# Token-row joints of a two-layer decoder step: pair turns in one run, row 2 ahead of the first unit, diagonals on ScalarE, last pass waiting per weight block

## The chip, the core and the metric

The program runs on one core of a Trainium2 chip. The metric is the device time in microseconds from start to end of one execution; a lower time is better. A profiled execution gives the trace, with the start and duration of every instruction on TensorE (PE), VectorE (DVE), ScalarE (ACT), GpSimd (POOL) and the queue of SyncE (SP).

## What is computed

Two layers over 512 prompt tokens and 64 new tokens (8 sequences of 8). Layer 0 mixes tokens by latent attention (MLA), layer 1 by gated linear attention (GLA). Around each mixer stands a half-step FFN before and after, each with a norm before and after.

```python
def rmsnorm(x, g):
    xf = x.astype(jnp.float32)
    y = xf * lax.rsqrt(jnp.mean(xf * xf, axis=-1, keepdims=True) + EPS)
    return (y * g.astype(jnp.float32)).astype(x.dtype)

def ffn_half(h, g_pre, g_post, w_in, w_out):
    a = rmsnorm(h, g_pre) @ w_in
    gate, up = jnp.split(a, 2, axis=-1)
    return h + FFN_RESID * rmsnorm((jax.nn.silu(gate) * up) @ w_out, g_post)
...
    for i in range(DEPTH):
        g = norm_g[i]
        yp = ffn_half(yp, g[0], g[1], ffn_w_in[i, 0], ffn_w_out[i, 0])
        ...
        yp = yp + rmsnorm(mp, g[3])
        ...
        yp = ffn_half(yp, g[4], g[5], ffn_w_in[i, 1], ffn_w_out[i, 1])
```

The width is 1024, the FFN's inner width 2816. All is float32.

## The kernel before

Six stages run one after the other: ffn, mla, ffn, ffn, gla, ffn. The residual h lies in SBUF by token rows, in five tiles: 0 to 3 of 128 prompt tokens each, 4 with the 64 new ones. They are worked in the order 0, 1, 4, 2, 3. Each stage first needs x = h times the pre-norm gain, transposed, so that the contraction lies on the partitions. The norm's own factor 1/sqrt(sum of squares) is applied later, when results leave PSUM.

Every product of float32 numbers is made from three matmuls of type fp32r: x is split in x_hi and x_lo, the weights in w_hi and w_lo, and hi x hi, lo x hi and hi x lo are added in PSUM. Weights come in blocks of 512 KB through four slots. SyncE loads a block into raw, ScalarE makes w_hi from it (split, L588), GpSimd makes w_lo (L972); for the second block of a stage VectorE does that (w_low, L1106). A slot is loaded again when TensorE has used its block.

A stage ends with its output projection (out_phase). Its output y is made in two halves of 512 columns. In the second half the last three blocks (the last pass) are worked tile by tile, so that the tiles end one after the other. For each finished tile ScalarE squares y (y_square, L602 to L607) and takes the root (y_root, L615); VectorE applies the post-norm gain (y_gain, L1115), inverts the root and adds the result to h (update, L1142). 

A joint is what lies between this and the next stage's dense work:

- **Turning.** TensorE transposes h (turn_pair, L1723, for tiles 0 and 1 together, two k of 128 columns at a time; turn_row, L1735, for the tiles 4, 2 and 3) into PSUM banks 6 and 7. ScalarE makes x_hi from the bank (high, L641), VectorE x_lo (low, L1080). A bank can be turned into again when x_lo has been taken from it.
- **First units.** A unit is one block of weights against 256 tokens (half 0: tiles 0 and 1) or 320 (half 1: tiles 2, 3 and 4). It goes to one of six ring banks. in_head works units 0, 1 and 2 of half 0, and then those of half 1.
- **Factors.** ScalarE squares the rows of h (h_square, L629) and takes the root (h_root, L635 and L636). VectorE inverts it and makes a diagonal matrix (diag, L1152). TensorE spreads it over all partitions with a matmul (spread_factors, L1744 and L1746), and VectorE copies it out (r_pre, L1159 and L1162) ahead of the first unit's eviction (L1195).

The order of instructions on each engine is the order in which they are written; an engine executes its own in that order, and waits for semaphores between. Semaphores are s_hnew (updates of h), s_turn, s_xhi, s_xlo, s_hi and s_lo (weights), s_used and s_unit (blocks and units done), s_evicted (banks freed) and s_diag. In the GLA stage the output projection waits for g_olo, which counts the lowered parts of its input: first the eight of tiles 0 and 1, then the eight of the others with x_s, the part of the new tokens (L1641, L1643).

## Time and profile before

| | us |
|---|---|
| three runs | 2522.61, 2524.40, 2524.88 |
| median | 2524.4 |
| the profiled execution | 2524.44 |
| its span, first to last instruction | 2522.4 |
| TensorE matmuls busy | 2415.3 (96%) |
| TensorE weight loads busy | 2186.4 (87%) |
| VectorE, ScalarE, GpSimd busy | 858.4, 795.7, 834.1 (34%, 32%, 33%) |

The mean granted clock of TensorE is 0.988 of full speed. Matmul rows overlap, since the duration of one has its way through the array in it; the distance between two starts is what one costs. In a waits view a line names who waited for whom; in a timeline the brackets give the idle time of the engine before the group and what ended it. A group of a timeline is merged from consecutive like instructions (x8).

### The profile page before, as it was taken

Reading aid. Unit: us, or ns where it says so; the run is one execution under the profiler, and the core shown is the slowest. Engines: PE = TensorE matmul, PEld = TensorE weight load, DVE = VectorE, ACT = ScalarE, POOL = GpSimd, SP = SyncE. Lnnn points to the kernel's source line nnn. Section 1 sums busy time; section 2 is a strip of 40 time slices with the busy share of each in tenths; the row PEclk is TensorE's granted clock in tenths of the full one; section 3 lists DMA queues with packets and bytes.
Section 4 is the critical chain, followed back from the end, with each engine's and each line's share of the span. In section 5 each row is a group of like instructions: output and inputs, shape, how many; then the busy total and the mean of one; then the engine's idle time right before and its main releaser. Section 6 shows DMA issues by size and latency. Waiting matters only on the chain.

```text
span 2522.4 us, 40060 instructions
## 1 busy us (share of the span) xinstructions
PE 2415.3 (96%) x15520; PEld 2186.4 (87%) x15520; DVE 858.4 (34%) x1923; ACT 795.7 (32%) x1604; POOL 834.1 (33%) x442
## 2 busy tenths in 40 slices
PE   7999999899999899999989999998999998999998
PEld 7999988786556799998879999887999778999987
DVE  4223200586431532320043222004465634332201
ACT  5222222414332532222243222224322434222222
POOL 3333333230212143333314333331344223333332
PEclk9999999999998999999999999999999999999999
DMA  3222222231541132222213222221211422222222
GB/s 115 84 84 83 91 83 68 67 113 51 170 140 43 42 93 84 83 91 84 84 42 100 78 82 91 84 84 52 86 59 52 158 61 74 84 83 83 88 80 87
DMA packets 65401, 211.91 MB, mean 84 GB/s; under 512 B 8348, under 2 KB 17053, under 8 KB 65022
## 3 DMA queue, kind: packets, MB, share of 16 engines
q1 hardware_dynamic: 62206, 199.70, 25.5%
q0 software_dynamic: 3072, 10.49, 1.5%
q8 instruction: 87, 1.43, 0.2%
q14 instruction: 36, 0.29, 0.0%
HBM read 202.34 MB, written 7.82 MB: 83 GB/s over the span
## 4 chain that ended last, share of the span: by engine, by line
PE 87%; DVE 5%; ACT 3%; issue 2%; POOL 1%; DMA 1%; POOLq 0%; SPq 0%; DVEq 0%; ACTq 0%
PE psum L1682 18%; PE psum L1683 17%; PE psum L1684 17%; PE psum L1810 7%; PE psum L1812 7%; PE psum L1811 7%; PE psum L1804 2%; PE psum L1803 2%; POOL w_lo L972 1%; PE psum L2012 1%; PE psum L2075 1%; PE psum L2157 1%; PE psum L1994 1%; ACT w_hi L588 1%; PE psum L1948 1%
## 5 line engine op out<-in xcount | busy, mean ns | idle before, releaser
L972 POOL TENSOR_TENSOR w_lo<-raw,w_hi 128x1024 fp32r<-128x1024 f32 (+1 forms) x317 | 758.9, 2397 | 1439.9 <-ACT w_hi L588 1439.8
L1682 PE MATMUL psum<-x_hi,w_hi 128*128 128x320 f32 (+1 forms) x3312 | 991.4, 299 | 23.4 <-POOL w_lo L972 23.4
L1683 PE MATMUL psum<-x_lo,w_hi 128*128 128x320 f32 (+1 forms) x3312 | 985.6, 298 | 0.0
L1684 PE MATMUL psum<-x_hi,w_lo 128*128 128x320 f32 (+1 forms) x3312 | 985.5, 298 | 0.0
L1682 PEld LDWEIGHTS psum<-x_hi,w_hi 128*128 128x128 f32 x3312 | 634.5, 192 | 27.0 <-POOL w_lo L972 24.6
L1683 PEld LDWEIGHTS psum<-x_lo,w_hi 128*128 128x128 f32 x3312 | 634.5, 192 | 0.4
L1684 PEld LDWEIGHTS psum<-x_hi,w_lo 128*128 128x128 f32 x3312 | 634.2, 191 | 0.0
L588 ACT ACTIVATE w_hi<-raw 128x1024 fp32r<-128x1024 f32 (+1 forms) x323 | 339.7, 1053 | 877.0 <-DMA raw<-ffn_out 377.1
L1195 DVE TENSOR_TENSOR work<-psum,r_pre 128x256 f32<-128x256 f32 (+1 forms) x352 | 160.3, 457 | 658.5 <-PE psum L1684 656.3
L1810 PE MATMUL psum<-w_hi,gu_hi 128*128 128x512 f32 x704 | 276.0, 392 | 3.8 <-POOL w_lo L972 3.2
L1811 PE MATMUL psum<-w_hi,gu_lo 128*128 128x512 f32 x704 | 274.1, 389 | 0.0
L1812 PE MATMUL psum<-w_lo,gu_hi 128*128 128x512 f32 x704 | 274.0, 389 | 0.0
L1115 DVE TENSOR_TENSOR y<-psum,g_post 128x512 f32<-128x512 f32 x48 | 32.4, 687 | 558.0 <-ACT y L602 557.1
L1810 PEld LDWEIGHTS psum<-w_hi,gu_hi 128*128 128x128 f32 x704 | 132.1, 188 | 34.1 <-POOL w_lo L972 4.9
L1812 PEld LDWEIGHTS psum<-w_lo,gu_hi 128*128 128x128 f32 x704 | 132.1, 188 | 27.8
L1811 PEld LDWEIGHTS psum<-w_hi,gu_lo 128*128 128x128 f32 x704 | 132.2, 188 | 26.7
L667 ACT ACTIVATE gu_hi<-work 128x256 f32 (+1 forms) x176 | 72.2, 410 | 237.2 <-DVE work L1201 237.2
L663 ACT ACTIVATE work<-work 128x256 f32<-128x256 f32 (+1 forms) x176 | 76.4, 437 | 165.0 <-DVE work L1195 165.0
L1201 DVE TENSOR_TENSOR work<-work 128x256 f32<-128x256 f32 (+1 forms) x176 | 114.9, 653 | 35.5 <-ACT work L663 18.3
L1206 DVE TENSOR_TENSOR gu_lo<-work,gu_hi 128x256 f32 (+1 forms) x176 | 73.4, 419 | 39.9 <-ACT gu_s L669 39.9
L441 POOL DMA_DIRECT2D cache<-cache_r x64 | 34.6, 541 | 148.1 <-issue 138.2
L1080 DVE SCALAR_TENSOR_TENSOR x_lo<-psum,gain_s,x_hi 128x128 fp32r<-128x128 f32 (+2 forms) x192 | 56.5, 359 | 39.7 <-ACT x_hi L641 39.7
(278 smaller groups left out, 2187.4 us busy)
## 6 DMA issues: line engine op xcount, KB each, us to landing
raw<-ffn_in SPq DMA_DIRECT2D x176, 512.0 KB, 3.6
raw<-ffn_out SPq DMA_DIRECT2D x88, 512.0 KB, 3.6
raw<-gla_in SPq DMA_DIRECT2D x25, 512.0 KB, 3.6
cache<-cache SPq DMA_DIRECT2D x64, 160.0 KB, 2.5
cache<-cache_r POOLq DMA_DIRECT2D x64, 160.0 KB, 2.8
raw<-mla_wo SPq DMA_DIRECT2D x8, 512.0 KB, 3.5
raw<-gla_wo SPq DMA_DIRECT2D x8, 512.0 KB, 3.6
st_s<-state_gla SPq DMA_DIRECT2D x8, 512.0 KB, 5.5
```

Of the source, the lines that this page charges most:

```text
L588: act.activation(w_hi[slot][:, 0:w], raw[slot][:, 0:w], ACT.Copy).then_inc(s_hi, 1)
L663: act.activation(work[:, hf, 0:HW[hf]], work[:, hf, 0:HW[hf]], ACT.Silu).then_inc(s_silu, 1)
L972: pool.tensor_tensor(w_lo[slot][:, 0:w], raw[slot][:, 0:w], w_hi[slot][:, 0:w].bitcast(F32), ALU.subtract).then_inc(s_lo, 1)
L1195: dve.tensor_tensor(dst, bank[bk][0:r, 0:HW[hf]], r_pre[0:r, H[hf]], ALU.mult).then_inc(s_evicted, 1)
L1201: dve.tensor_tensor(work[:, 2 + hf, 0:w], work[:, hf, 0:w], work[:, 2 + hf, 0:w], ALU.mult).then_inc(s_gu, 1)
L1206: last = dve.tensor_tensor(gu_lo[:, pi, c], work[:, 2 + hf, 0:2 * P], gu_hi[:, pi, c].bitcast(F32), ALU.subtract)
L1682: pe.matmul(out, wh, xh, start=start, stop=False)
L1683: pe.matmul(out, wh, xl, start=False, stop=False)
L1684: return pe.matmul(out, wl, xh, start=False, stop=stop)
L1810: pe.matmul(dst, w[0], m[0], start=start, stop=False)
L1811: pe.matmul(dst, w[1], m[0], start=False, stop=False)
L1812: return pe.matmul(dst, w[0], m[1], start=False, stop=stop)
```

## The change

Nothing in the arithmetic changes, except which engine makes the diagonal. Five things move.

**Banks.** Pair turns 2 and 3 go to ring banks, those of the next stage's units 0 and 1, instead of waiting for banks 6 and 7. Row 2's second group goes to the ring bank of unit 3.

```diff
-        s_h_in = [sem(f"s_h_in{t}") for t in range(TILES)]
+        s_h_in = [sem(f"s_h_in{i}") for i in range(TILES + 2)]
...
+        def pair_bank(b, i):
+            return 6 + i if i < 2 else (first_unit[b] + i - 2) % RING
+        def row_bank(b, t, i):
+            if t == 4:
+                return 6
+            return 7 if i == 0 else 6 if t == 3 else (first_unit[b] + HEAD) % RING
+        def in_sems(t):
+            return (t, TILES + t) if t < 2 else (t,)
```

**Start (SyncE).** Tiles 0 and 1 of x are loaded in halves of 512 columns, the first halves ahead of the first block of weights.

```diff
+            for half in range(2):
+                for t in range(2):
+                    sp.dma_start(row(t)[:, half * OUT_W:(half + 1) * OUT_W],
+                                 io["x_t"][t, :, half * OUT_W:(half + 1) * OUT_W]).then_inc(s_h_in[in_sems(t)[half]], 16)
+                if half == 0:
+                    sp.dma_start(raw[0][:, :], io["ffn_in"][0, 0]).then_inc(s_raw[0], 16)
...
-                    load(b0 + j, w_in[f, j])
+                    if st > 0 or j > 0:
+                        load(b0 + j, w_in[f, j])
...
-                        for t in ORDER[0:3] if j == 0 else ORDER[3:]:
+                        for t in ORDER[2:3] if j == 0 else ORDER[3:]:
```

**ScalarE.** It squares row 0 right after its update, takes the pairs in two parts around the square of y tile 2, splits block 2 ahead of row 3's high parts, makes those ahead of the other squares, and makes the diagonals.

```diff
-                    act.wait_ge(s_h_in[t], 16)
+                    for x in in_sems(t):
+                        act.wait_ge(s_h_in[x], 16)
...
-                    act.wait_ge(s_ysq, N_UP * (b - 1) + TILES + 3)
+                    if i % 2 == 0 and t != 0:
+                        act.wait_ge(s_ysq, N_UP * (b - 1) + TILES + 3)
...
-            def high_pair(b):
+            def high_pair(b, i):
...
-                for k in range(DT):
-                    act.wait_ge(s_turn, N_TURN * b + k // 2 + 1)
-                    x_high(b, k, H[0], 6 + k // 2 % 2, k % 2 * 2 * P)
+                act.wait_ge(s_turn, N_TURN * b + i + 1)
+                for k in (2 * i, 2 * i + 1):
+                    x_high(b, k, H[0], pair_bank(b, i), k % 2 * 2 * P)
+            def spread_diag(b):
+                for t in range(TILES):
+                    r = rows_in(t)
+                    act.wait_ge(s_hrec, 2 * b + (1 if t < 4 else 2))
+                    act.activation(diag[0:r, t * P:t * P + r], ident[0:r, 0:r], ACT.Identity,
+                                   scale=h_r[0:r, t:t + 1]).then_inc(s_diag, 1)
...
-                        x_high(b, k, slice(t * P, (t + 1) * P), 7 - k // 4, k % 4 * P)
+                        x_high(b, k, slice(t * P, (t + 1) * P), row_bank(b, t, k // 4), k % 4 * P)
...
+                    if t == 0 and b < n_st:
+                        h_square(b, 0)
...
-                    high_pair(b)
+                    high_pair(b, 0)
+                    high_pair(b, 1)
...
+                    high_pair(b, 2)
+                    high_pair(b, 3)
...
-                for t in ORDER[0:4]:
+                split(n1 + 2)
+                high(b, 3, range(DT))
+                for t in ORDER[1:]:
...
-                high(b, 3, range(4))
-                split(n1 + 2)
-                high(b, 3, range(4, DT))
-                h_square(b, 3)
...
+                spread_diag(b)
...
+            high_pair(0, 0)
...
-            high_pair(0)
+            for i in range(1, 4):
+                high_pair(0, i)
...
-            for t in ORDER[0:3]:
-                h_square(0, t)
...
-            for t in ORDER[3:]:
+            for t in ORDER:
...
+            spread_diag(0)
```

**VectorE.** It lowers the pairs in two parts, around tile 2's update, lowers row 4 ahead of w_low, and makes no diagonals.

```diff
-            def low_pair(b):
-                for k in range(DT):
-                    dve.wait_ge(s_xhi, N_HI * b + k // 2 * 2 + 2)
-                    x_low(b, k, H[0], 6 + k // 2 % 2, k % 2 * 2 * P)
+            def low_pair(b, i):
+                dve.wait_ge(s_xhi, N_HI * b + 2 * i + 2)
+                for k in (2 * i, 2 * i + 1):
+                    x_low(b, k, H[0], pair_bank(b, i), k % 2 * 2 * P)
...
-                        x_low(b, k, slice(t * P, (t + 1) * P), 7 - k // 4, k % 4 * P)
+                        x_low(b, k, slice(t * P, (t + 1) * P), row_bank(b, t, k // 4), k % 4 * P)
...
-                dve.wait_ge(s_hrec, 2 * b + 2)
-                for t in range(TILES):
-                    r = rows_in(t)
-                    dve.tensor_scalar(diag[0:r, t * P:t * P + r], ident[0:r, 0:r], h_r[0:r, t:t + 1], None,
-                                      ALU.mult).then_inc(s_diag, 1)
...
-                    low_pair(b)
+                    low_pair(b, 0)
+                    low_pair(b, 1)
...
+                low_pair(b, 2)
+                low_pair(b, 3)
+                low(b, 4, range(DT))
...
-                low(b, 4, range(DT))
...
-            low_pair(0)
+            for i in range(4):
+                low_pair(0, i)
```

**TensorE.** All four pair turns stand at one place in tile 2's last pass; row 2 is turned ahead of unit 0, row 3 between units 1 and 2; the factors are spread after k = 6 and 7 instead of 3 and 5. The last pass waits for its blocks one by one. In the GLA stage the first two blocks are worked for tiles 0 and 1 first, and these wait only for the first eight parts of g_olo.

```diff
-            def row_ready(b, t):
+            def row_ready(b, t, half=None):
...
-                    pe.wait_ge(s_h_in[t], 16)
+                    for x in in_sems(t) if half is None else in_sems(t)[half:half + 1]:
+                        pe.wait_ge(s_h_in[x], 16)
...
-                row_ready(b, 0)
-                row_ready(b, 1)
+                row_ready(b, 0, i // 2)
+                row_ready(b, 1, i // 2)
...
-                    pe.wait_ge(s_xlo, N_HI * b + 2 * (i - 2) + 2)
+                    free(first_unit[b] + i - 2)
...
-                        last = pe.transpose(bank[6 + i % 2][:, c:c + P], row(t)[:, k * P:(k + 1) * P], ident[:, :])
+                        last = pe.transpose(bank[pair_bank(b, i)][:, c:c + P], row(t)[:, k * P:(k + 1) * P], ident[:, :])
...
-                    pe.wait_ge(s_xlo, N_HI * b + (6 if t == 4 else (8, 16)[i] if t == 2 else (20, 24)[i]))
+                    if (t, i) == (2, 1):
+                        free(first_unit[b] + HEAD)
+                    else:
+                        pe.wait_ge(s_xlo, N_HI * b + {(4, 0): 2, (2, 0): 4, (3, 0): 20, (3, 1): 16}[t, i])
...
-                        last = pe.transpose(bank[6 if t == 4 else 7 - i][:, j * r:(j + 1) * r], row(t)[:, k * P:(k + 1) * P],
+                        last = pe.transpose(bank[row_bank(b, t, i)][:, j * r:(j + 1) * r], row(t)[:, k * P:(k + 1) * P],
...
-                for k in range(DT):
-                    pe.wait_ge(s_xlo, N_HI * st + k + 1)
-                    unit_k(0, 0, k)
...
-                for k in range(DT):
-                    unit_k(1, 0, k)
-                    if k == 4:
+                for j in range(HEAD):
+                    if j < 2:
+                        pe.wait_ge(s_xlo, N_HI * st + 6 + 2 * j)
+                    for k in range(DT):
+                        if j == 0:
+                            pe.wait_ge(s_xlo, N_HI * st + max(k + 1, 6))
+                        unit_k(j, 0, k)
+                    if j == 1:
...
-                for k in range(DT):
-                    unit_k(2, 0, k)
...
-                    if k in (3, 5):
-                        spread_factors(st, k // 2 - 1)
+                    if k >= 6:
+                        spread_factors(st, k - 6)
...
-                for half in range(2):
-                    for i in range(nb if half == 0 else nb - OUT_TAIL):
+                def blocks(half, lo, hi, tiles, used):
+                    for i in range(lo, hi):
...
-                                ready(k)
-                            for t in ORDER:
+                                ready(tiles, k)
+                            for t in tiles:
...
-                        if i < nb - 1:
+                        if used and i < nb - 1:
...
-                pe.wait_ge(s_lo, n0 + 2 * nb)
+                first = 2 if stages[st] == "gla" else 0
+                blocks(0, 0, first, ORDER[0:2], False)
+                blocks(0, 0, first, ORDER[2:], True)
+                blocks(0, first, nb, ORDER, True)
+                blocks(1, 0, nb - OUT_TAIL, ORDER, True)
...
+                        if t == ORDER[0]:
+                            pe.wait_ge(s_lo, n0 + 2 * nb - OUT_TAIL + i // 2 + 1)
...
-                        if t == 2 and b < n_st:
-                            if i == 1:
-                                turn_pair(b, 0)
-                                turn_pair(b, 1)
-                            if i in (3, 5):
-                                turn_pair(b, (i + 1) // 2)
+                        if t == 2 and i == 1 and b < n_st:
+                            for j in range(4):
+                                turn_pair(b, j)
...
-                out_phase(st, (gu_hi, gu_lo, gu_s), lambda k: k == FT - 1 and pe.wait_ge(s_gulo, 2 * FT * (f + 1)))
+                out_phase(st, (gu_hi, gu_lo, gu_s), lambda tiles, k: k == FT - 1 and pe.wait_ge(s_gulo, 2 * FT * (f + 1)))
...
-                out_phase(st, (x_hi, x_lo, x_s), lambda k: pe.wait_ge(g_olo, DT + k + 1))
+                out_phase(st, (x_hi, x_lo, x_s), lambda tiles, k: pe.wait_ge(g_olo, (0 if tiles == ORDER[0:2] else DT) + k + 1))
```

What now stands where, in rows of the instruction order: line, operation, out<-in, shape, count. A number behind a buffer's name tells buffers apart.

TensorE in the last pass of stage 1, tile 2 (ident,h is a transpose of h, gu the input of the output projection), before:

```order
L1812 MATMUL psum<-w_lo_62,gu_hi 128x512
L1723 MATMUL psum<-ident,h 128x128 x8
L1810 MATMUL psum<-w_hi_63,gu_hi 128x512
L1811 MATMUL psum<-w_hi_63,gu_lo 128x512
L1812 MATMUL psum<-w_lo_59,gu_hi 128x512
...
L1723 MATMUL psum<-ident,h 128x128 x4
L1810 MATMUL psum<-w_hi_64,gu_hi 128x512
```

and with the change:

```order
L1851 MATMUL psum<-w_lo_62,gu_hi 128x512
L1759 MATMUL psum<-ident,h 128x128 x16
L1849 MATMUL psum<-w_hi_63,gu_hi 128x512
L1850 MATMUL psum<-w_hi_63,gu_lo 128x512
L1851 MATMUL psum<-w_lo_59,gu_hi 128x512
L1849 MATMUL psum<-w_hi_63,gu_hi 128x512
L1850 MATMUL psum<-w_hi_63,gu_lo 128x512
L1851 MATMUL psum<-w_lo_59,gu_hi 128x512
```

The two groups of four that stood between tile 2's later k steps are now with the first eight: sixteen transposes in a row.

TensorE where the last pass ends (L1812, after: L1851) and the next stage's units begin; before, around the end of unit 0:

```order
L1682 MATMUL psum<-x_hi,w_hi_65 128x256
L1683 MATMUL psum<-x_lo,w_hi_65 128x256
L1684 MATMUL psum<-x_hi,w_lo_61 128x256
L1735 MATMUL psum<-ident,h 128x128 x8
L1682 MATMUL psum<-x_hi,w_hi_66 128x256
```

with the change, around the beginning of unit 0:

```order
L1851 MATMUL psum<-w_lo_60,gu_hi 128x512
L1774 MATMUL psum<-ident,h 128x128 x8
L1717 MATMUL psum<-x_hi,w_hi_65 128x256
L1718 MATMUL psum<-x_lo,w_hi_65 128x256
L1719 MATMUL psum<-x_hi,w_lo_61 128x256
```

Row 2's eight transposes have moved from behind unit 0 to ahead of it.

ScalarE from the split of the next stage's second block on (w_hi<-raw is a split, x_hi<-psum a high part, junk<-h a square, h_r a root), before:

```order
L588 ACTIVATE w_hi_66<-raw_58 128x1024
L641 ACTIVATE x_hi<-psum,gain_s 128x128 x8
L629 ACTIVATE junk_91,h_ss<-h 128x1024
L629 ACTIVATE junk_90,h_ss<-h 128x1024
L629 ACTIVATE junk_91,h_ss<-h 64x1024
L629 ACTIVATE junk_90,h_ss<-h 128x1024
L641 ACTIVATE x_hi<-psum,gain_s 128x128 x4
L588 ACTIVATE w_hi_63<-raw_55 128x1024
L641 ACTIVATE x_hi<-psum,gain_s 128x128 x4
L629 ACTIVATE junk_91,h_ss<-h 128x1024
L635 ACTIVATE h_r<-h_ss,eps_d 128x4
L636 ACTIVATE h_r<-h_ss,eps_d 64x1
```

with the change:

```order
L609 ACTIVATE w_hi_66<-raw_58 128x1024
L664 ACTIVATE x_hi<-psum,gain_s 128x128 x8
L609 ACTIVATE w_hi_63<-raw_55 128x1024
L664 ACTIVATE x_hi<-psum,gain_s 128x128 x8
L652 ACTIVATE junk_90,h_ss<-h 128x1024
L652 ACTIVATE junk_91,h_ss<-h 64x1024
L652 ACTIVATE junk_90,h_ss<-h 128x1024
L652 ACTIVATE junk_91,h_ss<-h 128x1024
L658 ACTIVATE h_r<-h_ss,eps_d 128x4
L659 ACTIVATE h_r<-h_ss,eps_d 64x1
L679 ACTIVATE diag<-ident,h_r 128x128 x4
L679 ACTIVATE diag<-ident,h_r 64x64
```

The split of the third block has moved from behind four squares and half of row 3 to ahead of both; row 3's eight high parts stand together, four squares behind them, and the diagonals ahead of the next split.

VectorE from w_low on (x_lo 128x64 is row 4, h<-y is the update of row 3), before:

```order
L1106 TENSOR_TENSOR w_lo_62<-raw_58,w_hi_66 128x1024
L1080 SCALAR_TENSOR_TENSOR x_lo<-psum,gain_s,x_hi 128x64 x8
L1115 TENSOR_TENSOR y_0_92<-psum,g_post 128x512
L1134 RECIPROCAL y_r<-y_r 128x1
L1142 SCALAR_TENSOR_TENSOR h<-y_3_87,y_r,h 128x512
L1142 SCALAR_TENSOR_TENSOR h<-y_0_92,y_r,h 128x512
L1080 SCALAR_TENSOR_TENSOR x_lo<-psum,gain_s,x_hi 128x128 x16
```

with the change, from the second pair lowering on:

```order
L1116 SCALAR_TENSOR_TENSOR x_lo<-psum,gain_s,x_hi 128x256 x4
L1116 SCALAR_TENSOR_TENSOR x_lo<-psum,gain_s,x_hi 128x64 x8
L1142 TENSOR_TENSOR w_lo_62<-raw_58,w_hi_66 128x1024
L1151 TENSOR_TENSOR y_0_92<-psum,g_post 128x512
L1170 RECIPROCAL y_r<-y_r 128x1
L1178 SCALAR_TENSOR_TENSOR h<-y_3_87,y_r,h 128x512
L1178 SCALAR_TENSOR_TENSOR h<-y_0_92,y_r,h 128x512
L1116 SCALAR_TENSOR_TENSOR x_lo<-psum,gain_s,x_hi 128x128 x16
```

Row 4 is lowered ahead of w_low, and the pairs' second part stands right ahead of it.

## Rows read from the trace of the kernel before

**Rows 1.** Waits of TensorE: who waited for whom, total us, times, longest us.

```profile
PE psum L1682 <- POOL w_lo L972: 23.4, 6, 4.6
PE psum L1735 <- DVE x_lo L1080: 15.6, 18, 1.7
PE psum L1723 <- DVE x_lo L1080: 10.1, 6, 1.8
PE psum L1723 <- DMA h<-x_t: 10.0, 1, 10.0
PE psum L1810 <- POOL w_lo L972: 6.0, 6, 1.4
...
PE psum L1810 <- DVE x_s L1643: 5.1, 1, 5.1
```

**Rows 2.** Timeline, TensorE, joint 1: start, us, operation, count, idle before and releaser.

```profile
427.68 0.50 PE L1810 MATMUL psum<-w_hi,gu_hi 128*128 128x512 f32 x1 [0.97 <-POOL w_lo L972]
...
440.06 1.03 PE L1723 MATMUL psum<-ident,h 128*128 128x128 f32 x8
...
444.25 0.63 PE L1723 MATMUL psum<-ident,h 128*128 128x128 f32 x4 [1.79 <-DVE x_lo L1080]
...
451.55 0.28 PE L1682 MATMUL psum<-x_hi,w_hi 128*128 128x256 f32 x1
...
454.42 0.60 PE L1735 MATMUL psum<-ident,h 128*128 128x128 f32 x4
456.69 0.66 PE L1735 MATMUL psum<-ident,h 128*128 128x128 f32 x4 [1.67 <-DVE x_lo L1080]
...
467.17 0.58 PE L1682 MATMUL psum<-x_hi,w_hi 128*128 128x256 f32 x1 [4.57 <-POOL w_lo L972]
...
472.13 0.31 PE L1682 MATMUL psum<-x_hi,w_hi 128*128 128x320 f32 x1
```

**Rows 3.** Windows: stretch, busy us of PE, PEld, DVE, ACT, POOL, granted clock.

```profile
442.00:445.00 3.00, 1.21 (x9) 0.78 (x8) 2.89 (x6) 1.16 (x4) 0.00 (x0) 1.00 0.00 0
464.88:471.71 6.83, 4.54 (x21) 4.54 (x22) 4.50 (x11) 3.23 (x8) 4.61 (x2) 0.50 0.01 2
...
1311.39:1314.80 3.41, 3.41 (x19) 3.41 (x18) 2.73 (x4) 1.52 (x2) 2.37 (x1) 0.50 0.00 0
...
2014.53:2024.77 10.24, 5.39 (x13) 4.26 (x14) 7.26 (x28) 6.12 (x22) 2.04 (x1) 0.50 0.44 154
```

**Rows 4.** Timeline, ScalarE, joint 1.

```profile
452.79 1.04 ACT L588 ACTIVATE w_hi<-raw 128x1024 fp32r<-128x1024 f32 x1
455.06 1.14 ACT L641 ACTIVATE x_hi<-psum,gain_s 128x128 fp32r<-128x128 f32 x4 [1.22 <-PE psum L1735]
...
458.40 1.07 ACT L629 ACTIVATE junk<-h 128x1024 f32<-128x1024 f32 x1
...
463.56 1.07 ACT L588 ACTIVATE w_hi<-raw 128x1024 fp32r<-128x1024 f32 x1
```

**Rows 5.** Timeline, VectorE, joint 1.

```profile
437.76 1.42 DVE L1142 SCALAR_TENSOR_TENSOR h<-y,y_r,h 128x512 f32<-128x512 f32 x2
...
453.87 1.23 DVE L1106 TENSOR_TENSOR w_lo<-raw,w_hi 128x1024 fp32r<-128x1024 f32 x1 [3.26 <-ACT w_hi L588]
...
457.33 1.42 DVE L1142 SCALAR_TENSOR_TENSOR h<-y,y_r,h 128x512 f32<-128x512 f32 x2
```

**Rows 6.** DMA issues: count, KB each, median us to landing.

```profile
raw<-mla_down SPq DMA_DIRECT2D x6, 512.0 KB, 4.3
```

**Rows 7.** Timeline, GpSimd, joint 1.

```profile
464.77 2.35 POOL L972 TENSOR_TENSOR w_lo<-raw,w_hi 128x1024 fp32r<-128x1024 f32 x1 [30.89 <-ACT w_hi L588]
```

**Rows 8.** Groups of instructions by line and shape.

```profile
L1152 DVE TENSOR_SCALAR diag<-ident,h_r 64x64 f32<-64x64 f32 x6 | 14.2, 2369 | 0.0
```

**Rows 9.** Timeline, VectorE, ahead of the GLA output projection.

```profile
2014.14 2.76 DVE L1641 TENSOR_TENSOR x_lo<-og,x_hi 128x256 fp32r<-128x256 f32 x8
```

**Rows 10.** Timeline, TensorE, start of the kernel.

```profile
17.16 0.58 PE L1682 MATMUL psum<-x_hi,w_hi 128*128 128x256 f32 x1
```


## Prediction

> **What bounds the kernel now.** I read the waits of TensorE first, then one joint between two stages in the timelines of all engines. TensorE is busy for 96% of the span, so only what it waits for, or what it does at half clock, can be taken away. Its waits [rows 1] are few, and most stand at the five joints, which look alike. In the first of them [rows 2] TensorE stops 1.79 us before the third pair turn, 1.67 us and twice briefly around the turns of rows 2 and 3, and 4.57 us before the third unit, whose low half of the weights (w_lo) comes from GpSimd. Of the totals in [rows 1] the start of the kernel holds 0.5 of the 23.4, 1.4 of the 15.6 and 1.1 of the 10.1 us. What is left for five joints is 22.9 + 14.2 + 9.0 = 46.1 us, 9.2 us each. Behind the 4.57 us the granted clock is 0.50 in every joint [rows 3]: for 4.5 us of matmuls in the first (busy 4.54 of 6.83 us; the two others that begin so read alike), for 3.41 us in the third and the fourth. Half of that is lost: 3 x 2.2 + 2 x 1.7 = 10.0 us. Outside the joints stand six waits for the last weight block ahead of the last pass (6.0 us), one before the GLA output projection (5.1 us) and the first rows of x (10.0 us).
>
> **The change, at one joint.** Times are on the clock of the trace of before, first joint.
>
> *Tail.* The last pass waits for one block at a time; tile 0's first four k steps come ahead of the last block, which was 0.97 us late. From 427.68 to 440.06 stand 54 matmuls [rows 2], 0.229 us each, so those twelve take 2.7 us. All six waits go: 6.0 us. TensorE is then at the turning point at 440.06 - 0.97 = 439.1.
>
> *Pair turns.* All four pairs in a row need no x_lo any more, since pairs 2 and 3 go to banks that were emptied long before; the 1.79 us go. In their place comes a smaller wait. ScalarE now squares row 0 (1.07 us in [rows 4], of which the next instruction waits for 1.04) ahead of the square of y tile 1, and that delays the update of row 1. It ended at 437.76 + 1.42 = 439.2 [rows 5]. The chain starts 0.7 us sooner (TensorE is 0.97 us ahead, but ScalarE first finishes the split of the next stage's first block), so it ends at 439.2 - 0.7 + 1.04 = 439.5: a wait of 0.4 us, with bounds 0 and 1.0 us.
>
> *Row 2.* From 440.06 to the first unit at 451.55 TensorE has 9.7 us of work and the 1.79 us [rows 2]; with fewer stops between transposes and matmuls 9.5 us, so 449.0. Row 2 is turned there, one group behind the other, 0.85 us (four transposes take 0.60 us with their end). Its update is done at about 447, since it needs only pairs 0 and 1 lowered ahead of it. The 1.67 us, which came from low(4) behind w_low on VectorE, are gone. Unit 0 takes 454.42 - 451.55 = 2.87 us, to 452.8.
>
> *Unit 1.* Its w_lo is VectorE's, 1.14 us behind ScalarE's split, which stood at 452.79 [rows 4, 5]. The block is loaded when tile 3 has used its predecessor, now at about 445.6; such a load takes 4.3 us [rows 6], and ScalarE is free at 450.2. So the split ends at 451.3, w_lo is there at 452.5, and nothing waits. Unit 1 ends at 455.6. This margin is thin: 0.3 us.
>
> *Row 3 and unit 2.* Row 3 is updated 1.9 to 3.3 us after w_low's start (453.87 and 457.33 in [rows 5], less the 1.6 us of low(4), which now runs ahead), so until 454.6; four low parts of row 2 later, at 455.8, it can be turned: wait 0.1 to 0.2 us, done at 456.6. The split for unit 2 moves ahead of the squares: 453.3 to 454.4 instead of 463.56. GpSimd takes 2.35 us [rows 7], until 456.8 or, if it has to wait for VectorE's second half of the update, 457.0. Wait 0.4 us, unit 2 from 457.0 to 459.9. The second halves begin at 459.9 instead of 472.13. With this gap gone nothing lowers the clock, so the 10.0 us of half speed go too.
>
> *Factors.* ScalarE has high(3) until 458.6, four squares 4.2, two roots 0.5, VectorE's reciprocals 0.3, five diagonals 1.4 (a 128x128 piece on ScalarE in [rows 4], 1.14 us for four), so 465.0. TensorE asks for them behind k = 6. A k step of the second halves is six matmuls of 320 columns; from unit 0's 2.87 us for 24 of 256 that is 6 x 0.12 x 320/256 = 0.9 us, so at 459.9 + 7 x 0.9 = 466.2: hidden by 1.2 us. The split behind them ends at 466.1, GpSimd's part at 468.5, needed at 470.9: hidden by 2.4 us. On VectorE the last diagonal piece took 2369 ns [rows 8] beside GpSimd; ScalarE's pieces replace it, but TensorE did not wait for it, so this brings nothing. Turning, high and low work is the same in count; only its place moves.
>
> *Sum of a joint.* Gone 46.1 + 10.0; new waits 0.4 + 0.15 + 0.4 = 0.95 us each, -4.8; six restarts of the pipeline fewer (a first matmul takes 0.58 instead of 0.41 us) about 0.6 each, +3.0. Five joints: 54.3 us.
>
> **GLA output.** TensorE waited 5.1 us for x_s, the last thing lowered. Tiles 0 and 1 of the first two blocks need only x_lo of the first half, which VectorE makes from 2014.14 on [rows 9], 0.35 us a step. So TensorE starts at 2014.5 with eight parts, 24 matmuls or 5.5 us at full clock, and x_s is ready (2019.4) before they end. The clock stands at 0.50 from 2014.53 to 2024.77 with only 5.39 us of matmuls in it [rows 3]. It fell from the small matmuls and the wait ahead, which stay, so as much or more may now run at half. Gain 5.0 us, bounds 3.4 and 6.5.
>
> **Start.** The first unit began at 17.16 [rows 10]. The halves of rows 0 and 1 land earlier, so all pairs are lowered by 13.4, but row 2, which is now turned ahead of unit 0, comes with the same bytes ahead of it: about 13.5, and eight transposes at half clock take 1.94 us. Unit 0 starts at 15.4. The early 1.7 us count half (half clock), the waits for rows 3 and w_lo go (1.3 us), low work ahead of unit 1 shortens too: the second halves come 3.6 us sooner. There all five squares and a table load of 1.28 us stand ahead of the diagonals: TensorE waits 0.7 us at k = 6. Net 2.9 us, bounds 0.5 and 4.7.
>
> **Forecast.** 54.3 + 6.0 + 5.0 + 2.9 = 68.2 us off the profiled execution's 2524.44 us (span 2522.4 and 2.0 outside it, equal to the median 2524.4): **2456 us**.
>
> **Rivals.**
>
> *Port collision.* VectorE's update reads two SBUF operands, GpSimd's w_lo too. What a meeting costs is seen in [rows 8]: a piece of 64x64 took 2369 ns. In my schedule VectorE starts its second half of row 3's update at about 453.9 and GpSimd asks at 454.45, so GpSimd waits 0.2 us. If it came first, the update would end 2.1 us later, row 3 would turn at 458.4, and each joint would cost 2.3 us more: 2468; with the clock falling as well, another 1.7 each: 2476. For: the margin is 0.5 us in five places. Against: both chains start from the same split, so the distance is fixed. Chance 14%. The Trainium skill, SBUF — State Buffer, section Who interferes with whom, says that the one that issues first has the pair for the whole instruction and the other fully blocks; the trace agrees, since the six pieces took as long as one GpSimd instruction (2.35 us).
>
> *Clock.* Sixteen transposes and the wait make about 2 us without a matmul ahead of the tail's last parts. In before, 1.79 us of idle time and four transposes left the clock at 1.00 (first row of [rows 3]); the next longer gap, 4.57 us, lowered it. If the bunch lowers it, 3.41 us per joint run at half: 1.7 x 5 = 8.5 us, 2465. Chance 8%. The Trainium skill, TensorE: Matmul & The Clock Gate, Part 4, holds that transposes don't count as busy for the clock, which speaks for this rival; the trace leaves it open, since before never had more than eight in a row at a joint.
>
> *Loads too late.* The blocks of units 1 and 2 land after the tail that now runs faster; if they come 1 us later, each joint waits 1 us: 2461, with 2 us 2466. Chance 7%, inside the range.
>
> *The change doesn't carry.* What is saved is waited for at the fourth unit, whose w_lo has 2.4 us of margin, or at the factors. Were ScalarE 5 us later than I put it, 2.6 to 4 us a joint would come back: 2475. Chance 4%.
>
> *Slower.* The clock stays at half through each joint and beyond, as it did for 10.24 us at the GLA output [rows 3]. It decides the sign only from 68 us lost, which is 27 us of half-speed matmuls per joint; at 30 us each, 75 us are lost: 2531. Against: no fall at a joint lasted over 6.83 us. Chance 2%.
>
> **Chances and range.** Forecast 65%. Its own bounds are 2451 (no new waits, best start and GLA) to 2462. 8 in 10 need the clock and load rivals and most of the collision: **2449 to 2474**. A measurement here tells 0.2% (5 us) from nothing. Faster 96%, within 1%, slower 3%.
>
> **What would show it.** In the profile after: no wait of TensorE above 1 us at a joint; 16 transposes in one row of the timeline; a short wait for VectorE's h ahead of them (0.4 us); granted clock 1.00 in the joints; second halves about 20.8 us after the first pair turn instead of 32. The waits for w_lo ahead of the last pass are gone. Wrong would be: h L1142 stretched to over 2 us beside GpSimd (collision), granted clock 0.50 in the tail (clock), a wait for w_lo of 1 us or more at units 1 to 3 (loads, no carry), or a start no sooner than 31 us for the first second half.

## The result and the profile after

| | before | after |
|---|---|---|
| median beside each other (4 runs each) | 2523.84 | 2453.01 us |
| runs | | 2456.59, 2456.14, 2449.88, 2449.62 |
| ratio | | 0.972, 95% interval 0.9701 to 0.9739 |
| the profiled execution, its span | 2524.44, 2522.4 | 2456.59, 2454.9 us |
| mean granted clock | 0.988 | 0.993 |

The changed kernel is 2.8% faster. The forecast, made against the profiled execution, was 2456 us.

Waits of TensorE after: who waited for whom, total us, times, longest us.

```profile
PE psum L1759 <- DMA h<-x_t: 9.2, 2, 5.9
...
PE psum L1759 <- DVE h L1178: 2.9, 5, 0.8
...
PE psum L1849 <- DVE x_s L1490: 1.4, 1, 1.4
...
PE psum L1783 <- ACT diag L679: 0.7, 1, 0.7
PE psum L1849 <- DVE x_lo L1675: 0.6, 1, 0.6
PE psum L1774 <- DMA h<-x_t: 0.5, 1, 0.5
```

Of [rows 1] only the wait for x from memory is left. The waits for GpSimd's w_lo (23.4 and 6.0 us), those for x_lo at the turns (15.6 and 10.1) and the 5.1 us for x_s (L1643) at the GLA output are gone; the x_s in the list (L1490) belongs to the MLA stage and stood in before too. New are 2.9 us for VectorE's updates of h, 0.7 for the diagonals (at the start) and 0.6 for the first x_lo at the GLA output.

TensorE at joint 1, after (timeline: start, us, operation, count, idle time before and releaser), to be held against [rows 2]:

```profile
435.94 1.94 PE L1759 MATMUL psum<-ident,h 128*128 128x128 f32 x16 [0.65 <-DVE h L1178]
437.63 0.47 PE L1849 MATMUL psum<-w_hi,gu_hi 128*128 128x512 f32 x1
...
442.60 0.71 PE L1774 MATMUL psum<-ident,h 64*128 64x64 f32 x8
...
445.42 1.03 PE L1774 MATMUL psum<-ident,h 128*128 128x128 f32 x8
...
452.27 1.06 PE L1774 MATMUL psum<-ident,h 128*128 128x128 f32 x8
```

Sixteen transposes stand in one row, and behind the 0.65 us ahead of them no row down to the second halves has an idle time. But the ends of matmuls are modelled, and a short wait can hide behind them. The starts show two. Row 2's eight transposes are followed by unit 0 after 0.79 us, row 3's by unit 2 after 1.11, and the weight loads (PEld) name the reason:

```profile
452.24 0.86 PEld L1774 LDWEIGHTS psum<-ident,h 128*128 128x128 f32 x8 [0.23 <-issue]
453.38 0.19 PEld L1717 LDWEIGHTS psum<-x_hi,w_hi 128*128 128x128 f32 x1 [0.28 <-POOL w_lo L1008]
```

So TensorE waits 0.3 us for w_lo ahead of unit 2, in all five joints (1.4 us in the waits of the weight loads). Ahead of row 3's turning it stops for about 0.2 us: the first transpose starts 0.34 us after the matmul before it, where 0.12 us is the usual distance. The view names no releaser for that; VectorE makes the x_lo parts of row 2 that this turning waits for from 451.00 on, the first four until about 452.1.

The second halves begin at 456.36, 20.41 us after the first transpose; in before, at 472.13, 32.07 us after it. The other joints read 20.47, 20.47, 20.44 and 20.47 us against 32.00, 31.56, 31.55 and 31.97.

VectorE and GpSimd there, after:

```profile
447.74 1.23 DVE L1142 TENSOR_TENSOR w_lo<-raw,w_hi 128x1024 fp32r<-128x1024 f32 x1 [0.90 <-ACT w_hi L609]
...
449.67 1.42 DVE L1178 SCALAR_TENSOR_TENSOR h<-y,y_r,h 128x512 f32<-128x512 f32 x2
451.00 2.15 DVE L1116 SCALAR_TENSOR_TENSOR x_lo<-psum,gain_s,x_hi 128x128 fp32r<-128x128 f32 x8
```

```profile
450.86 2.47 POOL L1008 TENSOR_TENSOR w_lo<-raw,w_hi 128x1024 fp32r<-128x1024 f32 x1 [20.54 <-ACT w_hi L609]
```

The update of row 3 keeps its 1.42 us; GpSimd starts 0.2 us before its end and takes 2.47 instead of 2.35 us [rows 7]. Granted clock (windows: stretch, busy us of PE, PEld, DVE, ACT, POOL, clock), first joints 1 and 3, then the GLA output:

```profile
435.00:457.00 22.00, 21.24 (x149) 18.94 (x148) 17.95 (x48) 15.79 (x47) 2.47 (x1) 1.00 0.30 90
...
1256.00:1278.00 22.00, 21.30 (x148) 18.87 (x147) 17.96 (x48) 15.72 (x46) 2.47 (x1) 1.00 0.23 73
...
1966.81:1970.22 3.41, 3.07 (x7) 2.51 (x8) 3.41 (x12) 1.51 (x5) 0.00 (x0) 0.50 0.86 306
```

The clock stays at its upper level (2.4 GHz) at all five joints, where it had stood at half in every one [rows 3]. At the GLA output it is at half (1.2 GHz) for 3.41 us instead of 10.24.

### The profile page after: what moved, and what is told of

It is laid out like the page before. It is cut to its first block, busy times and chain, and to the rows that moved or that the text cites. A ratio compares the mean times of both kernels' runs of the same rounds, so it can differ in the third digit from the quotient of the medians.

```text
span 2454.9 us, 40090 instructions
## 1 busy us (share of the span) xinstructions
PE 2403.7 (98%) x15520; PEld 2178.6 (89%) x15520; DVE 843.1 (34%) x1893; ACT 802.9 (33%) x1634; POOL 835.4 (34%) x442
## 3 DMA queue, kind: packets, MB, share of 16 engines
q8 instruction: 87, 1.43, 0.2%
## 4 chain that ended last, share of the span: by engine, by line
PE 88%; DVE 5%; ACT 3%; issue 1%; DMA 1%; POOL 1%; SPq 0%; DVEq 0%; ACTq 0%; POOLq 0%
PE psum L1717 18%; PE psum L1718 18%; PE psum L1719 18%; PE psum L1849 7%; PE psum L1850 7%; PE psum L1851 7%; PE psum L1842 2%; PE psum L1843 2%; PE psum L2119 1%; PE psum L2056 1%; PE psum L2201 1%; PE psum L2038 1%; ACT y L623 1%; DVE y L1151 1%; PE psum L1992 1%
## 5 line engine op out<-in xcount | busy, mean ns | idle before, releaser
L1851 PE MATMUL psum<-w_lo,gu_hi 128*128 128x512 f32 x704 | 273.9, 389 | 0.0
L1851 PEld LDWEIGHTS psum<-w_lo,gu_hi 128*128 128x128 f32 x704 | 132.2, 188 | 27.6
L1842 PE MATMUL psum<-w_hi,gu_s 128*128 128x512 f32 x176 | 68.5, 389 | 0.0
```

The source lines that it names most:

```text
L1842: pe.matmul(bank[u % RING], xs[:, k, :], wh, start=start, stop=False)
L1851: return pe.matmul(dst, w[0], m[1], start=False, stop=stop)
```

## The experiments

All but one begin from the changed kernel; each is named in brackets as it is called elsewhere in the text. Times are medians, ratios are to the kernel before on the same chip. Two runs of one kernel can lie 5 to 7 us apart (see f0_changed_again), so differences below that are read from the waits and starts in the traces, and the medians only bear them out or don't.

**One wait for the three last blocks** (e1_one_wait)

```diff
+                pe.wait_ge(s_lo, n0 + 2 * nb)
...
-                        if t == ORDER[0]:
-                            pe.wait_ge(s_lo, n0 + 2 * nb - OUT_TAIL + i // 2 + 1)
```

> The changed kernel, but TensorE again waits for all three last weight blocks ahead of the last pass (six places). Theory: block-by-block waiting gave what the waits of before show, 6.0 us in all, but not the whole comes back: while TensorE waits, ScalarE and VectorE go on, and the wait for row 1's update ahead of the pair turns (0.65, 0.77, 0.58, 0.58, 0.32 us) shrinks by about 0.3 us a joint. So +4.5 us against the changed kernel, waits for w_lo of 0.6 to 1.4 us ahead of the last pass. Rival (the weights come early enough anyway since the joints are shorter): no such waits, 0 us.

Measured: 2458.36 us, ratio 0.9742 (0.9722 to 0.9763). Its waits:

```profile
PE psum L1849 <- POOL w_lo L1008: 6.1, 6, 1.4
```

The six waits are back to a tenth of a microsecond. The wait for h is no longer in the list: TensorE comes to the turning point later, when row 1 is ready. So by the waits block-by-block waiting is worth 6.1 - 2.9 = 3.2 us in this kernel, since part of the lead that it gives is waited off again at the first pair turn. The median is 5.3 us over the changed kernel's (5.5 by the ratios), nearer to the 4.5 expected; the 2 us beyond the waits are within the scatter of one kernel and stay open.

**Block-by-block waits alone, in the kernel before** (e8_before_block_waits)

```diff
-                pe.wait_ge(s_lo, n0 + 2 * nb)
...
+                        if t == ORDER[0]:
+                            pe.wait_ge(s_lo, n0 + 2 * nb - OUT_TAIL + i // 2 + 1)
```

> The kernel of before with one part of the change alone: the last pass waits block by block. Theory: the six waits of 6.0 us in all go and nothing takes their place, since row 1's update is ready 0.9 us ahead of the pair turn in before: -6 us against before, the five joints otherwise as they were (31.6 to 32.1 us from the first pair turn to the second halves). Rival: the chains of ScalarE and VectorE at the joints are not tied to TensorE, and a later wait grows by what is saved here: under -3 us.

Measured: 2516.52 us (10 runs) against 2519.89 (13 runs), ratio 0.9987 (0.9977 to 0.9996). In its trace the six waits of [rows 1] are gone and the other waits stand at 23.4, 15.6, 10.1 and 5.1 us, as before. The waits bear out 6.0 us; the medians show 3.4, with an interval from 1 to 5.8, so the whole 6.0 doesn't reach the time. Neither forecast fits: no later wait grew, but the joints were not as before either. They take 32.39, 31.53, 31.99, 32.28 and 32.38 us, 1.4 more in all, with the clock at half for 30.7 instead of 27.3 us in them. All ten runs have a mean granted clock of 0.987 to 0.989, eleven of the thirteen beside them 0.991 to 0.993. The two of before at 0.987 and 0.988 took 2523.07 and 2524.62 us, over 3.8 us more than any of the ten. So at equal clock the saving is there, and half speed takes a part of it back. Whether the edit itself brings the lower clock isn't shown.

**Diagonals on VectorE again** (e2_diag_vector)

```diff
-                spread_diag(b)
...
+                dve.wait_ge(s_hrec, 2 * b + 2)
+                for t in range(TILES):
+                    r = rows_in(t)
+                    dve.tensor_scalar(diag[0:r, t * P:t * P + r], ident[0:r, 0:r], h_r[0:r, t:t + 1], None,
+                                      ALU.mult).then_inc(s_diag, 1)
```

> The changed kernel, but VectorE makes the diagonals again, right behind its reciprocals. Theory: they are off the path. VectorE would start them at 459.99 in joint 1 as ScalarE does, four pieces of 0.28 us, and the last one is held by GpSimd's subtraction until about 463.6; TensorE asks for it at 463.4. So a wait of 0.2 us at most in each joint, within 1 us in all. Rival (the held piece counts): each joint waits for the whole of GpSimd's instruction, +2.4 us each, +12 us.

Measured: 2455.93 us, ratio 0.9733 (0.9711 to 0.9754). Groups of instructions by shape (busy us, mean ns), VectorE in this kernel and then ScalarE in the changed one:

```profile
L1186 DVE TENSOR_SCALAR diag<-ident,h_r 64x64 f32<-64x64 f32 x6 | 14.4, 2393 | 0.0
```

```profile
L679 ACT ACTIVATE diag<-ident,h_r 64x64 f32<-64x64 f32 x6 | 2.0, 333 | 0.0
```

The slow last piece is back, and the joints stay at 20.41 to 20.47 us: it is off the path there. The median is 2.9 us over the changed kernel's, within the scatter of one kernel. Only at the start does TensorE wait for diagonals, 1.6 us in two waits (0.7 with ScalarE).

**Square of row 0 one tile later** (e3_square0_later)

```diff
-                    if t == 0 and b < n_st:
+                    if t == 1 and b < n_st:
                         h_square(b, 0)
```

> The changed kernel, but ScalarE squares row 0 behind the root of y tile 1 instead of ahead of the square of y tile 1. Theory: this square is what TensorE waits for ahead of the pair turns; it then lies in ScalarE's idle time (1.5 us ahead of the copy of y tile 4), row 1's update ends at about 434.3 instead of 435.8, and the five waits (2.9 us in all) go. -2.9 us against the changed kernel, nothing new. Rival (another wait stands right behind it, such as tile 4's update or the banks): the sum of waits at the joints stays, 0 us.

Measured: 2447.74 us, ratio 0.9703 (0.9682 to 0.9725). The wait for h is not in the list any more, and the joints take 20.39 to 20.40 us. So the square ahead of y tile 1's is what held row 1's update, as the prediction had it. The median is 5.3 us lower (4.3 by the ratios), of which the waits account for 2.9.

**GLA output over all tiles at once** (e4_gla_all_rows)

```diff
-                first = 2 if stages[st] == "gla" else 0
+                first = 0
```

> The changed kernel, but the GLA output projection waits again for the parts of all rows (no block is worked for tiles 0 and 1 first). Theory: the 5.1 us wait for x_s returns, and half-speed matmuls stay about as they are: +5 to +6 us against the changed kernel. Rival (the idle time only moves the clock's fall): less than +3 us.

Measured: 2458.54 us, ratio 0.9745 (0.9725 to 0.9765), 5.5 us over the changed kernel's median (6.3 by the ratios). Its waits:

```profile
PE psum L1849 <- DVE x_s L1677: 5.2, 1, 5.2
```

The wait of [rows 1] is back with its old size, and the clock stands at half for 6.83 us from 1963.92 on.

**Third split behind three squares and half of row 3** (e5_split_behind_squares)

```diff
                 high(b, 2, range(DT))
-                split(n1 + 2)
-                high(b, 3, range(DT))
-                for t in ORDER[1:]:
+                for t in ORDER[1:4]:
                     h_square(b, t)
+                high(b, 3, range(4))
+                split(n1 + 2)
+                high(b, 3, range(4, DT))
+                h_square(b, 3)
```

> The changed kernel, but ScalarE takes the order of before for the third block: three squares and four high parts of row 3 ahead of its split. Theory: unit 2 waits for w_lo of this block, which is ready at 453.3 in joint 1, just as TensorE asks (453.38). Three squares (3.1 us) put ScalarE at row 3, which is turned at 452.8; four high parts until 454.1, split until 455.1, GpSimd until 457.6: unit 2 starts 4.2 us later, TensorE is idle for about 4.5 us and the granted clock falls to 0.50 behind it as in before, 1.7 to 2.2 us more. Five joints: +30 us against the changed kernel, bounds 20 and 33. Rival (row 3's turning or the banks bound unit 2 as well): under +10 us, no fall of the clock.

Measured: 2481.56 us, ratio 0.9847 (0.9831 to 0.9863). Its waits, and TensorE in the timeline at joint 1:

```profile
PE psum L1719 <- POOL w_lo L1010: 21.2, 5, 4.2
```

```profile
457.38 0.58 PE L1719 MATMUL psum<-x_hi,w_hi 128*128 128x256 f32 x1 [4.23 <-POOL w_lo L1010]
```

The joints take 25.9 to 26.9 us, and in each the clock is at half for 3.41 or 6.83 us. This one place in ScalarE's order is worth 28.5 us by the medians (32 by the ratios) of the whole 70.8. The five joints of the trace are 30.2 us longer: 21.2 us of waits, the other 9 mostly half speed behind them.

**Third split ahead of row 2's high parts, so that GpSimd comes first** (e6_split_first)

```diff
                 split(n1 + 1)
+                split(n1 + 2)
                 high(b, 2, range(DT))
-                split(n1 + 2)
```

> The changed kernel, but ScalarE splits the third block right behind the second, ahead of row 2's high parts. This provokes the port collision of the prediction: GpSimd's subtraction then starts at about 449.5 in joint 1, VectorE asks for the first half of row 3's update (two operands from SBUF) at 449.7. Theory: the update is held until GpSimd ends at 451.9, ends itself at 453.3, row 2's low parts follow, row 3 is turned 2.2 us late, and each joint is 2.1 us longer: +10.5 us, bounds 8 and 15 (the clock may fall). Rival (the two engines share nothing here): the update keeps its 1.42 us, and the joints stay as they are, 0 to +1 us.

Measured: 2467.37 us, ratio 0.9788 (0.9771 to 0.9804). VectorE and GpSimd at joint 1, and the wait of TensorE:

```profile
449.77 3.26 DVE L1178 SCALAR_TENSOR_TENSOR h<-y,y_r,h 128x512 f32<-128x512 f32 x2
```

```profile
449.41 2.41 POOL L1008 TENSOR_TENSOR w_lo<-raw,w_hi 128x1024 fp32r<-128x1024 f32 x1 [19.05 <-ACT w_hi L609]
```

```profile
PE psum L1774 <- DVE x_lo L1116: 10.6, 6, 2.3
```

GpSimd began 0.36 us ahead of the update, and the update took 3.26 instead of 1.42 us: it ended 1.2 us after GpSimd did. TensorE waited for what comes behind. Joints without a fall of the clock take 22.00, 22.24 and 21.94 us, the two with one 23.42 and 23.78:

```profile
848.56:851.97 3.41, 3.41 (x19) 3.41 (x18) 2.42 (x10) 3.19 (x11) 0.00 (x0) 0.50 0.02 5
```

So the port collision is real. The edit also puts row 2's high parts behind the split, but those are done at 451.34 in joint 1, and VectorE comes to them only at 452.95, behind the stretched update; they are not what TensorE waits for. The collision costs 1.6 us a joint where I had said 2.3, and 1.4 to 1.8 more where the clock falls. In joint 1 row 3 is turned 18.2 us after the first transpose instead of 16.3, but w_lo for unit 2 is now early, and the 0.3 us for it fall away. In the changed kernel GpSimd starts 1.2 us behind the update, and the update is not touched.

**Start: weights first** (e7_start_weights_first)

```diff
+            sp.dma_start(raw[0][:, :], io["ffn_in"][0, 0]).then_inc(s_raw[0], 16)
-            for half in range(2):
-                for t in range(2):
+            for t in range(2):
+                for half in range(2):
...
-            high_pair(0, 0)
             split(0)
-            for i in range(1, 4):
+            for i in range(4):
                 high_pair(0, i)
```

> The changed kernel, but at the start SyncE loads the first weight block ahead of rows 0 and 1 of x, as before, and ScalarE splits it first. Theory: all sixteen pair transposes then start at about 9.8 us and take 3.9 us at half speed, so rows 4 and 2 are turned by 16.5 and unit 0 starts about 0.9 us later: +1 us against the changed kernel, bounds 0.3 and 2. Rival: unit 0 waits for row 2's landing anyway (0.5 us wait in the changed kernel), and the order ahead of it is worth nothing, 0 us.

Measured: 2448.86 us, ratio 0.972 (0.9702 to 0.9738). That is 4.2 us less by the medians and nothing by the ratios, so only the trace can tell. The theory fell: this kernel starts later and is ahead soon after. TensorE at the start, the changed kernel and then this one:

```profile
5.93 1.94 PE L1759 MATMUL psum<-ident,h 128*128 128x128 f32 x8 [5.93 <-DMA h<-x_t]
11.17 1.94 PE L1759 MATMUL psum<-ident,h 128*128 128x128 f32 x8 [3.30 <-DMA h<-x_t]
13.04 1.11 PE L1774 MATMUL psum<-ident,h 64*128 64x64 f32 x8
14.65 1.97 PE L1774 MATMUL psum<-ident,h 128*128 128x128 f32 x8 [0.49 <-DMA h<-x_t]
16.27 0.56 PE L1717 MATMUL psum<-x_hi,w_hi 128*128 128x256 f32 x1
```

```profile
9.48 3.65 PE L1757 MATMUL psum<-ident,h 128*128 128x128 f32 x16 [9.48 <-DMA h<-x_t]
13.06 2.03 PE L1772 MATMUL psum<-ident,h 64*128 64x64 f32 x16
14.84 0.37 PE L1715 MATMUL psum<-x_hi,w_hi 128*128 128x256 f32 x1
```

Eight transposes of 128x128 took 1.94 us at first, sixteen 3.65; at the joints sixteen take 1.94. So the engine starts at half speed (the 1.2 GHz level). In this kernel sixteen run without a break, and the next sixteen (eight of 64x64, eight of 128x128) take 2.03 us together: they run at full speed, and the clock's records give full speed from 13.32 on (17.80 in the changed kernel). No matmul but transposes had run by then. Unit 0 begins 1.43 us sooner; 0.49 of that is the wait for tile 2, which is gone, the rest the faster transposes. The second halves start at 25.14 instead of 26.52. The traces with x first read 26.20 to 27.45 (eight of them), the two with weights first and no added transposes 25.14 and 25.80. Two things come with it: ScalarE's table load of 1.28 us, in the changed kernel at 7.10 ahead of its first x_hi, is at 0.90 here, where nothing waits; and the 0.7 us for diagonals give way to 0.5 us for w_lo.

**The changed kernel again** (f0_changed_again)

No edit.

> The changed kernel, unaltered, beside the two that follow. The theory that its times lie in two clusters because the stretches of half clock inside MLA and GLA fall differently from run to run expects 2450 to 2457 us, each run with its own mean granted clock (0.993 to 0.997), the slower ones with the lower. The rival, that the clusters belong to single chips or calls, expects five times within 2 us.

Measured: 2455.09, 2450.68, 2452.57, 2452.79 and 2450.07 us, at granted clocks 0.994, 0.996, 0.995, 0.994 and 0.996; median 2452.57, ratio 0.9719 (0.9704 to 0.9734). On one chip, in one series, the times cover the same 5 us, in the order of the clock, and not in two clusters. It is no property of single chips. The difference is large enough, too: estimated from these numbers, a mean clock lower by 0.003 over 2455 us is 15 us more at half, of which a busy engine loses 7. One place where the clock differs is inside MLA. Windows of the changed kernel's first profile, of its profile here, then of e3_square0_later (2444.59 us in its profiled execution, clock 0.997):

```profile
758.49:761.90 3.41, 3.40 (x17) 2.43 (x18) 1.06 (x4) 2.51 (x6) 0.00 (x0) 0.50 0.22 88
772.14:785.79 13.65, 12.24 (x44) 10.78 (x44) 0.69 (x1) 1.54 (x2) 2.37 (x1) 0.50 0.00 0
```

```profile
770.71:784.36 13.65, 12.13 (x44) 10.91 (x45) 0.69 (x1) 1.54 (x2) 2.36 (x1) 0.50 0.00 0
```

```profile
771.70:778.53 6.83, 5.42 (x19) 4.55 (x19) 0.69 (x1) 1.54 (x2) 2.36 (x1) 0.50 0.00 0
```

The changed kernel is at half speed there for 17.06 us in one execution and 13.65 in the other. In e3_square0_later, with no edit to this work, it is 6.83 us, and in e7_start_weights_first the clock isn't at half there at all.

**Square later and weights first, together** (f1_both)

The edits of e3_square0_later and e7_start_weights_first.

> The square of row 0 behind the root of tile 1 (as in e3_square0_later), and the first block of weights with its split ahead of x (as in e7_start_weights_first), together. The two sit in different places, so they should add: the five waits for h go (2.9 us) and the start's second halves begin at 25.1 instead of 26.5 us (1.4 us), 4.3 us less than f0_changed_again, about 2448 us. Rival: the wait for h only moves, to a later wait for w_lo or for h at row 2; then 1.4 us less, and the waits of TensorE show it.

Measured: 2448.51 us, ratio 0.9702 (0.9685 to 0.9719), 4.1 us under f0_changed_again. No wait for h; joints 20.39 to 20.40 us (20.41 to 20.46 beside it); second halves at the start from 25.80, against 27.45. By the traces the two add as expected: 2.3 us of waits for h are gone (f0_changed_again has 2.3, not 2.9), and 1.65 us at the start. The times alone don't show it: the intervals of this kernel and of f0_changed_again overlap, and e3_square0_later and e7_start_weights_first alone have medians of 2447.74 and 2448.86. Of the kernels here it is the one to keep because its trace has both gains.

**And 24 transposes to raise the clock** (f2_both_warm)

They stand ahead of the first pair turn and compute nothing that is used.

```diff
+                    pe.wait_ge(s_const, 32)
+                    for i in range(24):
+                        pe.transpose(bank[5][:, 0:P], ident[:, :], ident[:, :])
```

> f1_both with 24 additional transposes of the identity into a free bank ahead of the first pair turn, as soon as the constants have landed; their results are not used. Theory, that a run of transposes raises the clock: it stands at 1.00 before the pair turns, the sixteen of them take 1.6 to 1.9 instead of 3.65 us, unit 0 starts no later than 14.4 and the second halves at about 24.3 us, 0.5 to 1.5 us less than f1_both. Rival, that transposes don't raise it: unit 0 and the second halves as in f1_both, the pair turns 3.65 us, no gain.

Measured: 2447.79 us, ratio 0.9702 (0.9684 to 0.9719): no gain over f1_both. TensorE at the start, and two windows:

```profile
3.48 5.38 PE L1804 MATMUL psum<-ident 128*128 128x128 f32 x24 [3.48 <-DMA ident<-ident]
10.74 2.01 PE L1757 MATMUL psum<-ident,h 128*128 128x128 f32 x16 [1.88 <-DMA h<-x_t]
13.37 0.68 PE L1772 MATMUL psum<-ident,h 64*128 64x64 f32 x8 [0.61 <-DVE x_lo L1114]
15.11 1.12 PE L1772 MATMUL psum<-ident,h 128*128 128x128 f32 x8 [1.06 <-DMA h<-x_t]
15.96 0.49 PE L1715 MATMUL psum<-x_hi,w_hi 128*128 128x256 f32 x1
```

```profile
9.22:16.05 6.83, 3.63 (x33) 3.22 (x34) 3.23 (x8) 4.57 (x13) 0.45 (x1) 1.00 1.01 332
16.05:19.46 3.41, 3.41 (x19) 3.41 (x18) 2.33 (x12) 3.41 (x15) 1.93 (x1) 0.50 0.31 123
```

The mechanism is as the theory says: behind 24 unused transposes the sixteen pair turns take 2.01 us, where f1_both has 3.65. The gain is not. The faster turning only runs into the next two waits (x_lo, then tile 2 from memory), TensorE is busy for 3.63 of 6.83 us, the clock falls again at 16.05, and unit 0 begins at 15.96 instead of 15.49 with its matmuls at half speed until 19.46. The second halves start at 27.03 instead of 25.80.

## Why the prediction was right

| term | predicted | measured |
|---|---|---|
| five joints | 54.3 | 54.0 |
| tail waits | 6.0 | 6.0 |
| GLA output | 5.0 | 6.1 |
| start | 2.9 | 3.8 |
| sum | 68.2 | 69.9 |
| span | | 67.5 |

**Joints.** From first pair turn to second halves five joints took 159.15 us before and 102.26 after, 56.9 less; ahead of that stand the new 2.9 us. The three new waits all came, at about the sizes that I gave them: 0.58 us a joint for row 1's update (0.4 predicted), 0.2 ahead of row 3 (0.15) and 0.3 for unit 2's w_lo (0.4), the last two visible only in the starts and the weight loads. That is 5.4 us where I had 4.8. 46.1 + 10.0 - 5.4 leaves 50.7, so the restarts that fall away have 3.3 us (3.0 predicted), if half speed gave back its 10.0, which no run separates. The 0.6 us a joint for them doesn't follow from the figures beside it: six times 0.17 is 1.0. That this term fits is partly luck. The schedule itself was met closely: relative to the first transpose I had row 2 at 9.5 us (9.48), row 3 at 16.3 (16.33), unit 2 at 17.5 (17.44) and the second halves at 20.4 (20.41). The 20.8 us among the prediction's signs counts the wait of 0.4 us ahead of the first transpose with it.

**Tail.** Right as a term of waits, and the two experiments show its two faces: alone 6.0 us of waits, of which the medians show 3.4, and in the changed kernel 3.2 net by the waits.

**GLA output.** The mis-sized term. I let as much or more run at half clock as before; it was 3.41 us with 3.07 us of matmuls in it instead of 10.24 with 5.39. 5.13 us of waiting became 0.56, and 6.1 us were saved, inside the bounds of 3.4 and 6.5: 4.6 us of waiting, the rest mostly less half speed.

**Start.** Unit 0 began at 16.27 (I had 15.4), since tile 2 could be turned only from 14.65 on, not from 13.5. The second halves began at 26.52, 4.6 us sooner, less 0.7 for the diagonals as predicted. At the first joint TensorE comes to the turning point 3.8 us sooner (435.29 instead of 439.09, each without its wait). What I had missed is the clock: the records give full speed from 17.80 instead of 21.15.

**From 69.9 to 67.5.** The clock inside the mixers took back the rest. In MLA 20.5 us ran at half instead of 17.1: besides the 13.65 us that both have, 543.45 and 758.49 after, 560.46 before, 3.41 us each. Inside GLA it was 6.83 us (1727.88) instead of 3.41 (1779.01). Half of each is lost, 1.7 us twice, 3.4 in all where the sums leave 2.4 to explain; 1.0 us stays unassigned. One kernel's runs differ by more than that (see f0_changed_again), so nothing ties this to the change.

**Rivals.** The port collision didn't happen, and e6_split_first shows that it would have cost about what was said: 14.4 us over the changed kernel (17 by the ratios), between my 12 (2468) and 20 (2476); its joints alone are 11.1 us longer, with the clock falling in two of the five. The order on VectorE and GpSimd decides, with the margin that the profile shows: the update begins at 449.67, GpSimd at 450.86. The Trainium skill, SBUF — State Buffer, section Who interferes with whom, has the later one fully blocked. The trace nearly agrees: the update took 3.26 us, its own 1.42 and 1.84 of the 2.05 for which GpSimd still ran. The clock didn't fall from sixteen transposes with 0.65 us of idle time ahead: 1.00 at all joints. The page TensorE: Matmul & The Clock Gate, Part 4, of the Trainium skill holds that transposes don't count as busy; for the float32 transposes of this kernel the starts of e7_start_weights_first and f2_both_warm contradict that, since there nothing but transposes ran before the engine was at full speed. No load was late: in joint 1 unit 1's w_lo is ready at 448.97, 0.20 us ahead of the unit's start at 449.17 (0.3 predicted), and unit 2 waits for GpSimd, not for a load. What was saved was not waited for again: the diagonals of joint 1 ended at 461.5, the joint having begun 3.5 us sooner than in my account (465.0), and TensorE asked for them at 462.5. Nor did the clock stay at half at any joint.

## What to carry to other kernels

When an engine stands at the head of a long queue, look in the order of its helpers first: one split moved ahead of three squares and half of row 3's high parts was worth some 30 us here, while work that nobody waits for at the joints (the diagonals) could be moved for nothing. Waits of 0.2 or 0.3 us don't appear among TensorE's matmuls; look at its weight loads and at the distances between starts. A wait of some microseconds also costs clock: price it with the half speed behind it, and let removed waits earn that back. A lead that is gained early is only kept as far as the next wait, so the pieces of a change are to be priced in their new surroundings.

## What the runs showed that was not expected

- **Transposes raise TensorE's clock.** Sixteen in a row from 9.48 us on had the engine at full speed by 13.32 us; in the changed kernel, with breaks of 3.30 and 0.49 us between the transposes, it was there only at 17.8, where matmuls go from 0.21 to 0.12 us apart.
- **Full clock is lost again if the engine then waits.** After the 24 unused transposes it fell at 16.05 us with TensorE busy for 3.63 us of the 6.83 before.
- **The granted clock in the profile reads 1.00 in the first microseconds** while the transposes there take twice their time (1.94 us for eight at 5.93 us, 1.03 for eight at 445.42). At the start durations are to be trusted, not that number. The changed kernel's window:

```profile
0.00:10.00 10.00, 1.94 (x8) 1.57 (x8) 0.39 (x6) 2.88 (x4) 0.21 (x5) 1.00 0.73 200
```

- **The same kernel varies by 5 to 7 us of 2450**, the slower runs with the lower mean clock. In two profiles of the changed kernel the stretches at half clock between 758 and 786 us, inside MLA, add up to 17.06 and 13.65 us; in two kernels that leave this work alone they are 6.83 and 0. Why a given execution gets the short or the long one stays open.
